# One loop body for all sixteen experts: six weight slots, gates spread per expert, in a two-layer hybrid diffusion step on one core

## What is computed

```python
def expert_choice_ffn(h, w_router, w1, w3, w2):
    B, L, D = h.shape
    cap = EC_CAPACITY * L // N_EXPERTS          # 64 of 512, 16 of 128
    aff = jax.nn.softmax((h @ w_router).astype(jnp.float32), axis=-1)
    gate, idx = lax.top_k(aff.transpose(0, 2, 1), cap)
    xs = jax.vmap(lambda hb, ib: hb[ib])(h, idx)
    a = jnp.einsum('becd,edf->becf', xs, w1)
    b = jnp.einsum('becd,edf->becf', xs, w3)
    y = jnp.einsum('becf,efd->becd', jax.nn.silu(a) * b, w2) * gate[..., None].astype(h.dtype)
    return jax.vmap(lambda yb, ib: jnp.zeros((L, D), yb.dtype).at[ib.reshape(-1)].add(yb.reshape(-1, D)))(y, idx)
```

## Time and profile before

| | |
|---|---|
| median of 3 runs | 2695.71 us (2691.11 to 2699.36) |
| profiled execution, its own time | 2696.3 us |
| its span | 2694.5 us |
| TensorE busy | 2520.7 us (94%) |
| TensorE weight loads busy | 1918.2 us (71%) |
| DVE / ScalarE / GpSimd busy | 1164.1 / 814.8 / 961.5 us |
| DMA | 572.39 MB, mean 212 GB/s |
| expert stage of layer 0 / layer 1, first to last block read | 865.55 to 1338.2 / 2186.92 to 2661.3 us |

### The profile page before, as it was taken

One profiled execution on the slowest core, in us unless ns is written; L12 is line 12 of the kernel. 1 busy time (PEld: TensorE's weight loads), 2 busy tenths in 40 slices (PEclk: granted clock), 3 DMA queues, 4 the chain that ended last, 5 costly groups with the idle time before them and its releaser, 6 DMA issues.

```text
span 2694.5 us, 79955 instructions
## 1 busy us (share of the span) xinstructions
PE 2520.7 (94%) x31456; PEld 1918.2 (71%) x31456; DVE 1164.1 (43%) x2031; ACT 814.8 (30%) x3454; POOL 961.5 (36%) x2976
## 2 busy tenths in 40 slices
PE   6999999999997999999889999999999969999995
PEld 3555676666755899888746566766666559988885
DVE  3998534555426111111278874345644341111114
ACT  3112223434214343333021132334331143433320
POOL 2374223232201255445535632133221014554444
PEclk9999999999999999999999999999999979999998
DMA  8332311112336899999723322111242249999993
GB/s 329 114 146 94 113 60 50 67 63 103 148 125 256 327 427 428 427 427 427 331 102 125 132 95 92 61 66 53 105 167 74 113 159 404 427 427 427 428 427 148
DMA packets 45134, 572.39 MB, mean 212 GB/s; under 512 B 5248, under 2 KB 7424, under 8 KB 9600
## 3 DMA queue, kind: packets, MB, share of 16 engines
q1 hardware_dynamic: 42336, 553.67, 50.7%
q10 hardware_dynamic: 2592, 16.38, 1.5%
HBM read 561.11 MB, written 8.91 MB: 212 GB/s over the span
## 4 chain that ended last, share of the span: by engine, by line
PE 67%; DMA 20%; DVE 10%; issue 2%; ACT 1%; DVEq 0%; POOL 0%; POOLq 0%; ACTq 0%
PE ps L511 50%; DMA ring<-in_w_exp 18%; PE ps L678 6%; DVE region_b L1707 5%; PE ps L933 3%; DMA ring<-in_w_last 2%; PE ps L899 1%; PE ps L882 1%; PE ps L870 1%; PE ps L1043 1%; DVE region_r L1996 1%; DVE rstd L1621 0%; DVE region_r L1995 0%; DVE region_r L1999 0%; PE ps L785 0%
## 5 line engine op out<-in xcount | busy, mean ns | idle before, releaser
L2321 POOL TENSOR_TENSOR region_m<-region_m,region_r 128x8 f32 x2416 | 424.1, 217 | 542.8 <-DVE region_r L2036 489.3
L511 PE MATMUL ps<-hT,ring 128*128 128x320 f32 (+2 forms) x1440 | 429.0, 440 | 8.4 <-ACT hT L1221 8.2
L2329 ACT ACTIVATE region_b<-hT 128x8 f32 x2400 | 290.6, 204 | 270.4 <-DVE region_r L2049 158.9
L511 PEld LDWEIGHTS ps<-hT,ring 128*128 128x128 f32 x1440 | 256.2, 191 | 145.0 <-issue 65.7
L511 PE MATMUL ps<-region_r,ring 128*64 128x80 f32 x7812 | 287.3, 233 | 22.2 <-DMA ring<-in_w_exp 19.3
L511 PEld LDWEIGHTS ps<-region_r,ring 128*64 128x64 f32 x7812 | 278.3, 137 | 28.9 <-DMA ring<-in_w_exp 25.8
L1707 DVE SCALAR_TENSOR_TENSOR region_b<-region_b,params 128x655 f32<-128x655 f32 x240 | 277.6, 1157 | 8.5
L511 PE MATMUL ps<-region_b,ring 128*128 128x320 f32 (+1 forms) x812 | 191.7, 373 | 0.5 <-DMA ring<-in_w_last 0.5
L511 PE MATMUL ps<-region_r,spare 128*64 128x80 f32 x4032 | 152.6, 237 | 27.9 <-DVE region_r L2331 18.1
L2167 POOL TENSOR_TENSOR params<-ring 128x512 f32<-128x512 f32 x32 | 41.9, 1310 | 372.2 <-DMA ring<-in_w_pair 370.7
L511 PEld LDWEIGHTS ps<-region_r,spare 128*64 128x64 f32 x4032 | 147.7, 140 | 32.0 <-DVE region_r L2331 18.6
(11 more groups left out here) (291 smaller groups left out, 3778.8 us busy)
## 6 DMA issues: line engine op xcount, KB each, us to landing
region_b<-in_w_exp SPq DMA_DIRECT2D x60, 2048.0 KB, 25.2
ring<-in_w_exp SPq DMA_DIRECT2D x60, 2048.0 KB, 25.3
ring<-in_w_mix SPq DMA_DIRECT2D x39, 2048.0 KB, 8.1
region_x<-in_w_exp SPq DMA_DIRECT2D x30, 2048.0 KB, 25.2
spare<-in_w_exp SPq DMA_DIRECT2D x30, 2048.0 KB, 25.3
ring<-in_w_pair SPq DMA_DIRECT2D x32, 1536.0 KB, 6.4
ring<-in_w_ada SPq DMA_DIRECT2D x4, 2048.0 KB, 10.3
x_store<-region_m ACTq DMA_DIRECT2D x2, 2560.0 KB, 10.6
```

What stands on the lines that cost most here:

```text
L511: ins = pe.matmul(*args, **kw)
L2321: last = eng.tensor_tensor(x[:, :, token], x[:, :, token], y_gated[e % 2][:, :, c:c + 1], ALU.add)
L2329: last = eng.activation(into[:, :, c:c + 1], h[:, :, token], ACT.Copy)
```

## The change

- All six blocks of an expert now stand in one loop body of 16 turns, in the order a, b, a, b, down, down, all of the same expert (`up_block`, `down_block`). Slots are 4, 1, 5, 2, 3, 0 (`EXP_SLOTS`) for all 96 blocks; slots 6 and 7 serve the modulation alone. The load of block n goes into the slot of block n - 6.
- A down block runs its 64 steps in two parts, first the four chunks that half 0 of the inner width has made, then the other four; the first down block waits for `b_used` between them. The two down blocks write two PSUM banks.
- Gates: DVE lays out one expert's gates (`lay_gates`), and one matmul per turn spreads them (`spread_gates(e)`).
- DVE's product goes straight into `act`. GpSimd adds all 80 columns of expert 14.
- ScalarE gathers 48 columns of the next expert ahead of its first silu and 32 ahead of the second (before 40 and 40).
- Top-k: the two context rounds stand ahead of the last latent round. The last columns of expert 0 are divided 3, 3 and 2 over ScalarE, DVE and GpSimd; ScalarE and GpSimd take the context columns, eight each, ahead of them.
- In layer 0 the modulation blocks 0 to 2 are loaded where expert blocks 0, 2 and 1 were, into slots 7, 6 and 3, and block 3 behind expert block 0. The second turn of affinities stands behind all modulation steps on TensorE.
- On the host side the expert weights are one array in the order of reading.

```diff
-FIRST_SLOTS = (7, 3, 6, 0)
-LOOP_SLOTS = (4, 1, 5, 2, 7, 3)
-AHEAD = 8
+ADA_SLOTS = (7, 6, 3, 0)
+EXP_SLOTS = (4, 1, 5, 2, 3, 0)
...
-                    if (name, p) == ("pair", 11):
-                        load_expert(0)
-                    if (name, p) == ("pair", 12):
+                    if l == 0 and (name, p) == ("pair", 11):
+                        load_next_ada(0)
+                    if l == 0 and (name, p) == ("pair", 12):
                         need("o_ready", 2 * PAIRS)
                         sp.wait_ge(kv_stored, 2 * 16 * (l + 1))
-                        load_expert(2)
+                        load_next_ada(1)
                     if (name, p) == ("pair", 13):
                         need("br_step", 56)
-                        load_expert(1)
+                        load_next_ada(2) if l == 0 else load_expert(4)
...
                 need("br_read", 32)
-                load_expert(4)
+                load_expert(0)
+                load_next_ada(3) if l == 0 else load_expert(5)
+                load_expert(1)
+                need("ctx_out_done", 2)
+                load_expert(2)
+                load_expert(3)
                 if l == 0:
-                    for n, b in enumerate(NEXT_ADA[:SLOTS]):
-                        load(BLOCK_AT[1][b], a["w_ada"][n])
...
+                    load_expert(4)
+                    load_expert(5)
-                for n in range(AHEAD, EXP_BLOCKS * NE):
+                for n in range(EXP_BLOCKS, EXP_BLOCKS * NE):
                     load_expert(n)
...
-                next_ada(("turn", 1), ("rows", 2))
+                next_ada(("turn", 1), ("rows", 2), ("turn", 2), ("rows", 3), ("turn", 3))
                 turn_affinities(2)
-                next_ada(("turn", 2), ("rows", 3), ("turn", 3))
...
+                def down_block(n, e, half):
+
+                    w = weights(EXP_AT[l] + n, e - 1)
+                    need("y_copied", 2 * e - 1 + half)
+                    for part in range(2):
+                        if part and not half:
+                            need("b_used", 2 * e + 1)
+                        for m in range(4):
+                            for k in range(part * KC // 2, (part + 1) * KC // 2):
+                                ins = expert_step(w, y_banks[half], act, m, k, (m, k) == (0, 0))
+                    ins.then_inc(S["y_done"], 1)
...
-                up_blocks(0, 0, 0, True)
-                spread_gates()
-                up_blocks(1, 2, 0, False)
-                with pe.Fori(1, NE) as e:
+                with pe.Fori(1, NE + 1) as e:
                     need("xs_ready", e)
-                    up_blocks(2 * e, FIRST_BLOCKS, e - 1, False)
-                    down_block(2 * e, FIRST_BLOCKS + 2, e - 1)
-                    up_blocks(2 * e + 1, FIRST_BLOCKS + 3, e - 1, False)
-                    down_block(2 * e + 1, FIRST_BLOCKS + 5, e - 1)
-                for b in range(LAST_BLOCKS):
-                    need("act_ready", HALVES)
-                    expert_block(FIRST_BLOCKS + LOOP_BLOCKS + b, 0, last_banks[b], act_last, "y_done")
+                    for half in range(2):
+                        need("sil_ready", 2 * e - 1 + half)
+                        up_block(2 * half, e - 1, a_ps, "a_done")
+                        need("b_used", 2 * e - 1 + half)
+                        up_block(2 * half + 1, e - 1, b_ps, "b_done")
+                    spread_gates(e)
+                    for half in range(2):
+                        down_block(4 + half, e, half)
...
+                v.sem_inc(S["xs_ready"], 1)
+                v.sem_inc(S["b_used"], 1)
+                v.sem_inc(S["y_copied"], 2)
+                for e in range(NE):
+                    for half in range(2):
+                        i = 2 * e + half
+                        need("b_done", i + 1)
+                        need("sil_ready", i + 2)
+                        v.tensor_tensor(flat(act)[:, half * HC:(half + 1) * HC], b_ps, sil[half], ALU.mult)\
+                            .then_inc(S["b_used"], 1)
+                    if e < NE - 1:
                         need("xs_parked", e + 1)
                         v.tensor_copy(flat(xs), flat(xs_next)).then_inc(S["xs_ready"], 1)
...
+                    copy_y(2 * e)
+                    copy_y(2 * e + 1)
+                    if e < NE - 1:
+                        lay_gates(e + 1)
```

More of the change, by code:

```diff
@@ L153 @@
     for _n in range(EXP_BLOCKS * NE):
-        take(FIRST_SLOTS[_n] if _n < FIRST_BLOCKS else LOOP_SLOTS[(_n - FIRST_BLOCKS) % EXP_BLOCKS], expert=(_l, _n))
+        take(EXP_SLOTS[_n % EXP_BLOCKS], expert=(_l, _n))
 def tile_count(phase, m):
@@ L608, in ada_turn @@
                         last = pe.transpose(ps[:, 1, m * P:(m + 1) * P], row[:, n % 2, m * P:(m + 1) * P], ident)
+                        if m == 0 and pending:
+                            last.then_inc(slot_used[pending.pop(0)], 1)
                     last.then_inc(S["ada_turned"], 1)
@@ L1127, in layer, with spread_gates, expert_step, up_block @@
                 turn_logits(2)
-                next_ada(("turn", 1), ("rows", 2))
+                next_ada(("turn", 1), ("rows", 2), ("turn", 2), ("rows", 3), ("turn", 3))
                 turn_affinities(2)
-                next_ada(("turn", 2), ("rows", 3), ("turn", 3))
[L1132 to L1144, removed]
+                def spread_gates(e):
+                    need("gates_laid", e)
+                    pe.matmul(gate_bank, ones[0:NE, :], gates_laid, start=True, stop=True).then_inc(S["gates_wide"], 1)
+                def expert_step(w, ps, moving, m, k, start):
+                    for at in range(0, P, WCOLS):
+                        ins = pe.matmul(
+                            ps[at:at + WCOLS, m * CAP:(m + 1) * CAP],
+                            w[:, k, m * P + at:m * P + at + WCOLS], moving[:, k, :],
+                            start=start, stop=k == KC - 1, tile_position=(0, at), skip_group_check=True)
+                    return ins
+                def up_block(n, turns, ps, done):
                     w = weights(EXP_AT[l] + n, turns)
@@ L1148, in expert_block @@
                         for k in range(KC):
-                            for at in range(0, P, WCOLS):
-                                z = (m, k, at) == (3, KC - 1, P - WCOLS)
-                                ins = (pe.matmul if z else mm)(
-                                    ps[at:at + WCOLS, m * CAP:(m + 1) * CAP],
-                                    w[:, k, m * P + at:m * P + at + WCOLS], moving[:, k, :],
-                                    start=k == 0, stop=k == KC - 1, tile_position=(0, at))
@@ L2027, in copy_y @@
                         need("y_added", e - 1)
-                    bank, first, _ = GATE_BANKS[e // 6]
-                    gates = bank[:, (e - first) * CAP:(e - first + 1) * CAP]
-                    y = PS[1][:, 0, 0:HC] if e < NE - 1 else last_banks[half]
-                    v.tensor_tensor(y_gated[e % 2][:, rows, :], y.rearrange("p (k c) -> p k c", k=4),
+                    v.tensor_tensor(y_gated[e % 2][:, rows, :], y_banks[half].rearrange("p (k c) -> p k c", k=4),
                                     token_gates[:, rows, :], ALU.mult).then_inc(S["y_copied"], 1)
-                    need("y_copied", j + 2)
@@ L2040, in layer @@
-                for i in range(HALVES):
-                    e, half = divmod(i, 2)
-                    need("b_done", i + 1)
-                    need("sil_ready", i + 1)
-                    if half == 0:
-                        into = sil[0] if e < NE - 1 else flat(act_last)[:, 0:HC]
-                        inc(v.tensor_tensor(into, PS[0][:, 1, 0:HC], sil[0], ALU.mult), "b_used")
-                    elif e < NE - 1:
+                v.sem_inc(S["xs_ready"], 1)
+                v.sem_inc(S["b_used"], 1)
```

156 lines of the change are left out of this document (57 added, 99 removed).

## The result

The changed kernel takes 2795.02 us (median of four runs, 2768.46 to 2799.32), the kernel before 2696.38 (four runs as well). The ratio, which goes by the means, is 1.0347, 95% interval 1.028 to 1.0415. It is slower by 3.5%, where 0.2% faster was forecast, and outside the range. The profiled execution took 2791.99 us, its span is 2790.2, 95.7 more than before.

The account below looks back on a forecast made before the run. Each expert stage was taken as DMA-bound, ending with its last landing. An earlier dense start saves 2.4 us in layer 0 and 2.8 in layer 1, together 5.2: 2690.5 us against the median, range 2681 to 2699.

Parts of the forecast that it names:

- R3: Rival: TensorE's expert loop code is fetched at every turn, six 1.16 us gaps an expert, 111 us, 2801; chance 0.04.
- Block 6 issued as block 0 is read, no hole: Head of each expert stage: each block read frees the next load's slot at once, so the gap in SP's loads goes.
- The start: Reordered top-k makes `xs` whole 0.85 us sooner (bounds 0.3 and 1.3): TensorE starts at 864.7, layer 1 at 2186.1.
- Gaps of 1.16 us in blocks 2 to 5, none later: TensorE's first pass over the loop's code: one wait for code behind dense loads per block, making each 5.6 us.
- +42.7: Layer 0, from TensorE's start: block 5 read at +33.7 issues block 11, whose load takes 9.0 us and lands then.
- 5.045 us a block from there: Steady stretch of each stage: DMA never lacks work, so 84 blocks after block 11 take 423.8 us.
- 2.4 us: Layer 0's expert stage: its last load lands at 1331.2, this much sooner than in the kernel before.
- 85 blocks in 430.4 us: Kernel before, layer 0: the time from block 10's landing at 903.2 to the last landing at 1333.56.
- Edits at nothing: Modulation block order, second affinities turn, GpSimd's 80 rows, per-expert gates, next layer's loads and down-block order were put at no cost.
- R2: Rival: silu, product and down blocks of one expert become a chain, TensorE idles; 54 us, 2745; chance 0.08.

Follow-up runs that it names:

- experiment 1: The changed kernel with both TensorE loops started at instruction 32 of a 16 KiB fetch block, nothing else: 2694.02 us, ratio 0.9993 to the kernel before.
- experiment 2: The changed kernel with both TensorE loops started at instruction 208 of a 16 KiB fetch block: 2688.9 us, ratio 0.9978 to the kernel before.
- experiment 5: The changed kernel with both TensorE loops started at instruction 238 of a 16 KiB fetch block: 2687.27 us, ratio 0.998 to the kernel before.

## Why the prediction was wrong, and where it was right

**The step that failed** is the one that put the fetching of the loop's code at nothing, in rival R3: "Rows 8 speak against it, for a body 0.3% shorter. Chance 0.04." In its place six returns of layer 1 fetched nine packets each, and the stage grew by 96.0 us. I read the earlier trace rows as a property of the loop: its code stays with the engine. It was a property of the loop at its place. What matters is how many 16 KB blocks the body touches; 1548 to 1554 instructions touch seven or eight, as the head stands. The change took straight blocks of code away ahead of the loop, and added instructions to the body, and layer 1's head moved from about slot 2 to slot 241. The question that the prediction put ("385 matmuls where it had 384") looked at six instructions in the body and not at the code that went or moved ahead of it. The rows of before could not have told the slot of the new head, so the chance should have been that of a throw: with 1554 instructions a head from 239 to 255 reaches over, 17 slots in 256; with layer 0's 15 that is by estimate a chance of 0.12, three times what I gave. A count of the built program would not have told it either as it was made here, since it gave 206 for a head at 241; the first-pass gaps of a trace do.

**The price of R3 was nearly right by luck.** 111 us were worked out from six gaps of 1.16 us in each of 30 turns, and 98.6 came. In truth no turn of layer 0 pays, and six of layer 1 pay 14 to 22 us each, some 11 of it in the two gaps at the head, from which the DMA's lead gives part back. The granted clock of 0.50 behind those gaps was in no term of it.

**The page that I set aside.** The Trainium skill, "Runtime: NRT & Kernel Launch", section "Instruction fetch mechanics", says that a taken branch whose target lies outside a window of two pages forces a fetch. By that every turn of both kernels would fetch. The traces don't agree: a body of seven blocks turned 15 times without being fetched again, with no packet on q8 from 2300 to 2650 us (experiments 1, 2 and 5). The same section also gives TensorE 128 KiB for instructions, 2048 of them; that is eight blocks of 16 KiB. That bound is near: seven blocks stayed, and bodies that touched eight were fetched again, in some turns. So the mechanism that the section names was the one to price, for a body of some 1550 instructions, and the prediction took the wrong one of its two bounds. Crossing a boundary is "mostly hidden", as the same section has it, at the first two of layer 0's first pass; at the four behind them, with the loads dense, it cost 0.93 to 1.91 us, and at the first behind a head that was fetched again 3.4 to 4.9.

**The expected gain, point by point**, in layer 0 of the changed kernel, which no fetch disturbs:

- *Block 6 issued as block 0 is read, no hole*: right. SP's queue, the loads of blocks 6 to 11, against the earlier trace rows:

```profile
871.21 0.33 SPq L423 DMA_DIRECT2D region_b<-in_w_exp  x1
875.63 0.33 SPq L423 DMA_DIRECT2D ring<-in_w_exp  x1
881.28 0.33 SPq L423 DMA_DIRECT2D region_x<-in_w_exp  x1
887.57 0.33 SPq L423 DMA_DIRECT2D ring<-in_w_exp  x1
893.68 0.33 SPq L423 DMA_DIRECT2D region_b<-in_w_exp  x1
900.28 0.33 SPq L423 DMA_DIRECT2D ring<-in_w_exp  x1
```

- *The start*: right in layer 0, 864.80 for 864.7, and not in layer 1, which starts at 2186.88, not 2186.1, and so gains nothing; with the loops placed at 208, 238 and 32 it was 2180.59, 2183.48 and 2189.12.
- *Gaps of 1.16 us in blocks 2 to 5, none later*: right in place and number, low in size. From the chain, same layer:

```profile
876.97 1.01 issue
...
882.62 1.59 issue
...
889.30 0.93 issue
...
894.88 1.91 issue
```

  1.36 us on average. A block behind such a gap also takes 4.64 to 4.70 us, not 4.43, and the one behind the gate matmul 5.18 with it, so that blocks 2 to 5 take 24.7 us together where 22.7 were forecast. Block 5 is read at +35.5, not +33.7; the load then takes 8.5 where I had taken 9.0, so block 11 lands at +44.0, not +42.7.
- *5.045 us a block from there*: 84 blocks from 908.8 to 1333.7 (1307.84 and 25.9 to landing) are 5.06 each. So layer 0 gains nothing where 2.4 us were forecast: 1.3 went at the head and 1.1 in the steady stretch. The second was an error of the sum: the prediction's own 85 blocks in 430.4 us are 5.063 each, and it set 5.045 against them.
- *Edits at nothing*: nothing in the traces speaks against them; R2 did not come, there is no gap of TensorE inside an expert of layer 0 beyond 1.2 us on a landing.

**With the fetches gone the time comes out in the forecast's range, in part by luck.** At slot 238 the changed kernel takes 5.7 us less than before, at 208 6.2, at 32 1.1; forecast were 5.2; the 1.1 can't be told from no change. What changed shows in the profiles, where TensorE starts and where the last load is issued: experiment 5, layer 1,

```profile
2183.48 6.03 PE L1123 MATMUL ps<-region_r,region_b 128*64 128x80 f32 x128 [12.55 <-DVEq L2019]
```

```profile
2623.43 0.33 SPq L423 DMA_DIRECT2D ring<-in_w_exp  x1
```

3.4 and 7.8 us sooner than before. From TensorE's start to the last issue layer 1 takes 444.3 us before, and 440.1, 440.0 and 440.7 at slots 208, 238 and 32. But the kernel before at slot 208 takes 441.3 (2186.33 to 2627.64), so most of these 4 us come with the place of the loop; at the same slot the change is worth 1.2 us in this stage and 2.9 in layer 0's (441.7 and 438.8). These are single traces, the one at 208 of its fastest run. When layer 1 begins differs too (2180.59 to 2189.12), and which piece of code makes the difference was not looked for. The versions at 208 and 238 beat the kernel before by 0.2%; that is below the 0.3% that I called measurable, but their intervals leave out 1.

**What stays open.** Why one instruction over brings one fetching turn, three bring six and four bring seven; why the old kernel at four over had three; and why never more than every second turn. The spread of the changed kernel's runs (2768 to 2799) would fit a number of such turns that differs from run to run, but only one of them has a trace.
